# GpSimd computes the low part of a weight slot in four pieces instead of one

## The chip, the cores and the metric

The kernel runs on one core of a Trainium2 chip. The metric is the device time of one execution in microseconds (us); lower is better. The core has five engines that run side by side and meet at semaphores: PE (TensorE, matrix products), DVE (VectorE), ACT (ScalarE), POOL (GpSimd) and SP (SyncE, which here only starts transfers). In the rows, PEld is PE's weight load.

## The reference

Two layers of a hybrid decoder step run over 256 prompt tokens and 64 batch tokens (8 sequences of 8). Cut to the order of the work, a layer is:

```python
x = x + 0.5 * swiglu(rmsnorm(x, ffn1_norm), ffn1_w_gate, ffn1_w_up, ffn1_w_down)
z = rmsnorm(x, mix_norm) @ w_in            # 1024 -> 2048: q | k | v | p | a, g | u, v
att = moba_attention(rms(q), rms(k), v)    # the batch tokens also see 256 cached keys
pool = trailing_means(p, (2, 4, 8, 16)) - p, then a map per group
conv = silu(layernorm(depthwise_conv31(a * sigmoid(g)))) @ conv_pw
gmlp = gelu(u) * (tril(spatial_w) @ rmsnorm(gelu(v)) + spatial_b)
x = x + concat(att, pool, conv, gmlp) @ w_out
x = x + 0.5 * swiglu(rmsnorm(x, ffn2_norm), ffn2_w_gate, ffn2_w_up, ffn2_w_down)
```

All of it is in float32.

## The kernel before

**The products.** Every float32 operand of a large product is split into a high part (rounded to fp32r) and a low part (the rest), and PE adds three products: high by high, high weight by low input, low weight by high input (lines 557, 558 and 560). Weights come in slots of 128 rows by 8 k-tiles of 128 columns (1024 columns; in the down projections 6 or 5 k-tiles). There are four slots, j = 0 to 3, each with a place for the raw weights (`raw`), the high part (`w_hi`) and the low part (`w_lo`). SP loads `raw[j]` when the low part made of its old content is done. ACT rounds it into `w_hi[j]` (line 836) when PE has finished with the slot. Then `w_lo = raw - w_hi` is computed, by DVE (line 1041) for most slots, and by POOL (line 468) for 16 slots of each layer: those of the last three of four iterations of the input projection (`BASE_I`, i = 1 to 3) and those of the first iteration of the output projection (`BASE_O`, i = 0). PE waits for the low part of a slot before its first product with it, and frees the slot after 24 products.

**The layer's middle.** Each engine has its own list of instructions, written out by hand, and no scheduler changes it. Between the last iterations of the input projection and the output projection stand the mixers. On POOL the order is: the 12 slots of the input projection; 16 instructions of the late convolution taps for the batch tokens (lines 485 and 488, the last of which PE's convolution mean, line 663, waits for); the window sums of the pooling mixer (lines 503 to 530); the 4 slots of the output projection.

On DVE, in the order in which they come: the copies of the normed q and k into `q_pad` and `k_all` (lines 1266 and 1267, six of them), the rest of the convolution taps (1153), the softmax of the prompt tokens, the gate's norm (1314, twice), the softmax of the batch tokens (`prob_s` by its inverse sum, 1320, then by a mask into `prob_new`, 1324), a product for the gates (1330), a reciprocal (1335), and the product of the convolution's layer norm (1338, twice), on which ACT's swish (993) waits.

On PE the mixers stand in this order: transposes of the gate values (687), prompt attention (701), transposes of the batch probabilities (731, which wait for line 1324), the spatial gates (710 to 720), batch attention (738, 741), the convolution's pointwise map (765, which waits for the swish of line 993), the pooling map (758), transposes (751), and then the output projection.

Semaphore `split_p` counts the slots that POOL has done: one for each slot. PE and SP both wait on it.

Of the kernel before, what the change touches and what calls it, by code (L numbers as in the profile page):

```python
# [24 lines left out]
F32 = mybir.dt.float32  # L25
F32R = mybir.dt.float32r
I32 = mybir.dt.int32
ALU = mybir.AluOpType
# [3 lines left out]
P = 128  # L32
# [11 lines left out]
DT = D_MODEL // P  # L44
# [41 lines left out]
CONST_LOADS = 2 + len(KEPT) + 4 + 2  # L86
GROUPS = 4

STORED_STEP, HISTORY_STEP = 7, 4
SMALLS = 7  # L90
STATES = 7
# [12 lines left out]
def hybrid_decoder(nc, xT, w8, w11, gains, vecs, consts, pool_w, conv_pw, sp_wT, sp_b,  # L104
# [3 lines left out]
    with ctx:  # L108
        place = [16512]

        def sb(name, shape, dt=F32, at=None):
            n = 4
            for s in shape[1:]:
                n *= s
            offset = place[0] if at is None else at[0]
            t = nc.alloc_sbuf_tensor_at(name, shape, dt, offset=offset)
            end = offset + (n + 31) // 32 * 32
            if at is None:
                place[0] = end
                assert end <= 229344, (name, end)  # L120
            else:
                at[0] = end
                assert end <= at[1], (name, end, at[1])
            return t

        raw = sb("raw", [P, 4, 8 * P])
        w_hi = sb("w_hi", [P, 4, 8 * P], F32R)
        w_lo = sb("w_lo", [P, 4, 8 * P], F32R)
# [93 lines left out]
        def sig(name, per_layer, head=0):  # L222
            return Signal(ctx.enter_context(nc.semaphore(name)), per_layer, head)
# [12 lines left out]
        split_p = sig("split_p", 16)  # L236
# [226 lines left out]
        def _(pool):  # L463
            def split_iteration(L, base, i):

                for j in range(4):
                    pool.wait_ge(split_hi.sem, L * split_hi.per + (base + i) * 4 + j + 1)
                    pool.tensor_tensor(w_lo[:, j, :], raw[:, j, :], w_hi[:, j, :].bitcast(F32), ALU.subtract).then_inc(split_p.sem, 1)  # L468

            def late_history_taps(L):  # L470

# [66 lines left out]
            for L in range(DEPTH):  # L538
                for i in range(1, IT_I):
                    split_iteration(L, BASE_I, i)  # L540
                late_history_taps(L)
                window_sums(L)
                split_iteration(L, BASE_O, 0)
# [973 lines left out]
```

## Time and profile before

| | us |
|---|---|
| median of three runs | 1189.28 |
| the runs | 1186.16, 1189.28, 1194.22 |
| the profiled execution, its own time | 1193.69 |
| its span in the trace | 1191.9 |
| PE busy in the span | 1161.5 (97%) |
| DVE busy | 754.6 (63%) |
| ACT busy | 528.0 (44%) |
| POOL busy | 120.1 (10%), 104 instructions |

The rows come from the profiled execution. Busy times of engines overlap. The three runs lie 8 us apart, which is what a difference has to be read against. Where a row names an engine and a line behind an arrow, the instruction waited for that.

### The profile page before, as it was taken

The page shows a single profiled execution, that of the slowest core. Times are in us where ns is not written, and L with a number is a line of the kernel's source. Part 1 is how long each engine was busy: PE and PEld are TensorE (multiplying, and loading weights), DVE is VectorE, ACT ScalarE, POOL GpSimd, SP SyncE. Part 2 cuts the span into 40 slices and gives each one's busy share as a digit, 9 for nine tenths or more (in the row PEclk, how much of TensorE's full clock was granted, in tenths as well). Part 3 has the DMA queues.
Part 4 walks back from the last instruction along what each step waited for, and adds up shares of the span by engine and source line. Part 5 has one row for each costly group of instructions (what it writes and reads, how often), then busy time and mean ns, then how long its engine had stood idle before and what let it go on. Part 6 is the DMA issues. An engine that isn't in the chain of part 4 may idle for free.

```text
span 1191.9 us, 22460 instructions
## 1 busy us (share of the span) xinstructions
PE 1161.5 (97%) x7920; PEld 1138.6 (96%) x7920; DVE 754.6 (63%) x1225; ACT 528.0 (44%) x778; POOL 120.1 (10%) x104
## 2 busy tenths in 40 slices
PE   5999999999899999999999999999998999999999
PEld 4999999999789999999999999999976999999998
DVE  6667765557967666555566677645778675666442
ACT  4444444444656344444444444444446453444332
POOL 1000000026810000000000000000576000000000
PEclk9999999999999999999999999999998999999999
DMA  7544434567236444435564444455652354444453
GB/s 245 176 143 155 143 114 146 148 195 233 83 107 188 150 150 150 146 111 145 167 205 155 144 151 132 127 153 171 205 189 72 109 173 144 153 146 136 129 151 104
DMA packets 71356, 180.23 MB, mean 151 GB/s; under 512 B 10074, under 2 KB 25234, under 8 KB 71314
## 3 DMA queue, kind: packets, MB, share of 16 engines
q1 hardware_dynamic: 70656, 178.97, 48.2%
q10 hardware_dynamic: 658, 0.73, 0.2%
q8 instruction: 23, 0.38, 0.1%
q14 instruction: 19, 0.16, 0.0%
HBM read 176.09 MB, written 3.58 MB: 151 GB/s over the span
## 4 chain that ended last, share of the span: by engine, by line
PE 91%; DVE 7%; issue 1%; DMA 1%; ACT 0%; SPq 0%; DVEq 0%; ACTq 0%
PE bank L557 30%; PE bank L560 30%; PE bank L558 30%; DVE bank L1153 1%; DMA x<-in_xT 1%; PE bank L765 0%; DVE prob_s L1320 0%; DVE w_lo L1041 0%; DVE xg_lo L1048 0%; DVE prob L1274 0%; DVE q_pad L1266 0%; DVE z_w L1314 0%; PE bank L570 0%; DVE prob L1300 0%; DVE tmp L1309 0%
## 5 line engine op out<-in xcount | busy, mean ns | idle before, releaser
L836 ACT ACTIVATE w_hi<-raw 128x1024 fp32r<-128x1024 f32 (+2 forms) x352 | 337.9, 961 | 464.6 <-PE bank L560 452.5
L557 PE MATMUL bank<-xg_hi,w_hi 128*128 128x320 f32 x1664 | 519.0, 312 | 11.5 <-DVE xg_lo L1048 11.5
L558 PE MATMUL bank<-xg_lo,w_hi 128*128 128x320 f32 x1664 | 515.3, 310 | 0.0
L560 PE MATMUL bank<-xg_hi,w_lo 128*128 128x320 f32 x1664 | 515.3, 310 | 0.0
L1041 DVE TENSOR_TENSOR w_lo<-raw,w_hi 128x1024 fp32r<-128x1024 f32 (+2 forms) x320 | 349.2, 1092 | 159.8 <-ACT w_hi L836 148.9
L557 PEld LDWEIGHTS bank<-xg_hi,w_hi 128*128 128x128 f32 x1664 | 313.6, 188 | 15.3 <-issue 12.4
L558 PEld LDWEIGHTS bank<-xg_lo,w_hi 128*128 128x128 f32 x1664 | 313.6, 188 | 0.9 <-issue 0.2
L560 PEld LDWEIGHTS bank<-xg_hi,w_lo 128*128 128x128 f32 x1664 | 313.4, 188 | 0.0
L557 PE MATMUL bank<-h_hi,w_hi 128*128 128x320 f32 x704 | 217.5, 309 | 0.0
L558 PE MATMUL bank<-h_lo,w_hi 128*128 128x320 f32 x704 | 217.5, 309 | 0.0
L560 PE MATMUL bank<-h_hi,w_lo 128*128 128x320 f32 x704 | 217.5, 309 | 0.0
L468 POOL TENSOR_TENSOR w_lo<-raw,w_hi 128x1024 fp32r<-128x1024 f32 x32 | 78.0, 2455 | 778.1 <-ACT w_hi L836 778.1
L557 PEld LDWEIGHTS bank<-h_hi,w_hi 128*128 128x128 f32 x704 | 132.2, 188 | 0.0
L558 PEld LDWEIGHTS bank<-h_lo,w_hi 128*128 128x128 f32 x704 | 132.2, 188 | 0.0
L560 PEld LDWEIGHTS bank<-h_hi,w_lo 128*128 128x128 f32 x704 | 132.2, 188 | 0.0
L1075 DVE TENSOR_TENSOR tmp<-bank,rms 128x320 f32<-128x320 f32 x88 | 43.2, 491 | 101.8 <-PE bank L560 101.8
L1072 DVE TENSOR_TENSOR tmp<-bank,rms 128x320 f32<-128x320 f32 x88 | 43.2, 491 | 54.2 <-PE bank L560 52.7
L821 ACT ACTIVATE xg_hi<-x,gain 128x320 fp32r<-128x320 f32 (+1 forms) x48 | 26.3, 561 | 82.3 <-DVE x L1098 81.8
L844 ACT ACTIVATE h_hi<-tmp 128x320 f32 (+1 forms) x88 | 41.5, 472 | 21.4 <-DVE tmp L1078 21.4
L1048 DVE SCALAR_TENSOR_TENSOR xg_lo<-x,gain,xg_hi 128x320 fp32r<-128x320 f32 (+1 forms) x48 | 27.2, 579 | 34.6 <-ACT xg_hi L821 34.6
L1078 DVE TENSOR_TENSOR tmp<-tmp 128x320 f32<-128x320 f32 x88 | 43.3, 492 | 5.0
L1153 DVE SCALAR_TENSOR_TENSOR bank<-conv_in,vec,bank 128x256 f32<-128x256 f32 x116 | 46.4, 479 | 0.0
(178 smaller groups left out, 707.9 us busy)
## 6 DMA issues: line engine op xcount, KB each, us to landing
raw<-in_w SPq DMA_DIRECT2D x224, 512.0 KB, 3.8
raw<-in_w SPq DMA_DIRECT2D x64, 384.0 KB, 3.1
raw<-in_w SPq DMA_DIRECT2D x64, 320.0 KB, 2.8
k_all<-in_cache_kT SPq DMA_DIRECT2D x32, 128.0 KB, 2.8
v_past<-in_cache_v SPq DMA_DIRECT2D x32, 128.0 KB, 3.2
x<-in_xT SPq DMA_DIRECT2D x2, 640.0 KB, 5.9
out_yT<-x SPq DMA_DIRECT2D x1, 960.0 KB, 4.9
out_kT<-qk SPq DMA_DIRECT2D x2, 320.0 KB, 4.7
```

Of the source, the lines that this page charges most:

```text
L468: pool.tensor_tensor(w_lo[:, j, :], raw[:, j, :], w_hi[:, j, :].bitcast(F32), ALU.subtract).then_inc(split_p.sem, 1)
L557: pe.matmul(out, hi, in_hi[:, k, :], start=first and n == 0, stop=False)
L558: pe.matmul(out, hi, in_lo[:, k, :], start=False, stop=False)
L560: mm = pe.matmul(out, lo, in_hi[:, k, :], start=False, stop=last and end)
L836: act.activation(w_hi[:, j, 0:count * P], raw[:, j, 0:count * P], ACT.Copy).then_inc(split_hi.sem, 1)
L844: act.activation(h_hi[:, bass.ds(i * 2 + m, 1), :].rearrange("p a t -> p (a t)"), tmp[:, 6 + m, :], ACT.Copy).then_inc(h_hi_ok.sem, 1)
L1041: dve.tensor_tensor(w_lo[:, j, 0:count * P], raw[:, j, 0:count * P], w_hi[:, j, 0:count * P].bitcast(F32), ALU.subtract).then_inc(split_v. ...
L1048: dve.scalar_tensor_tensor(out=xg_lo[:, bass.ds(d, 1), :].rearrange("p a t -> p (a t)"), in0=one, scalar=gain[:, bass.ds(gain_col, 1)], in ...
L1072: dve.tensor_tensor(tmp[:, m, :], bank[2 * m][:, 0:TOK], rms[:, :], ALU.mult).then_inc(taken.sem, 1)
L1075: dve.tensor_tensor(tmp[:, 4 + m, :], bank[2 * m + 1][:, 0:TOK], rms[:, :], ALU.mult).then_inc(taken.sem, 1)
L1078: dve.tensor_tensor(tmp[:, 6 + m, :], tmp[:, 2 + m, :], tmp[:, 4 + m, :], ALU.mult).then_inc(h_ok.sem, 1)
L1153: dve.scalar_tensor_tensor(out=out, in0=conv_in[:, c, bass.ds(k, SEQ)], scalar=vec[:, bass.ds(L * NV + k * GT + (V_CW + c), 1)], in1=conv_ ...
```

## The change

For each of POOL's 32 slots the one subtraction over 1024 columns becomes four subtractions over 256 columns each, in order, with nothing between them. The semaphore is counted by the last one, so that SP and PE are still told once, when the whole slot is done. Nothing else differs: the lists of the other four engines are the same, instruction for instruction.

```diff
+LOW_TILES = 2
...
                 for j in range(4):
                     pool.wait_ge(split_hi.sem, L * split_hi.per + (base + i) * 4 + j + 1)
-                    pool.tensor_tensor(w_lo[:, j, :], raw[:, j, :], w_hi[:, j, :].bitcast(F32), ALU.subtract).then_inc(split_p.sem, 1)
+                    for first in range(0, DT, LOW_TILES):
+                        cols = slice(first * P, (first + LOW_TILES) * P)
+                        low = pool.tensor_tensor(w_lo[:, j, cols], raw[:, j, cols], w_hi[:, j, cols].bitcast(F32), ALU.subtract)
+                    low.then_inc(split_p.sem, 1)
```

## Rows read from the trace of the kernel before

**Rows 1.** The page: the chain that ended last, by engine.

```profile
PE 91%; DVE 7%; issue 1%; DMA 1%; ACT 0%; SPq 0%; DVEq 0%; ACTq 0%
```

**Rows 2.** Groups of POOL instructions by shape: count, busy us, mean ns.

```profile
L468 POOL TENSOR_TENSOR w_lo<-raw,w_hi 128x1024 fp32r<-128x1024 f32 x32 | 78.0, 2455 | 778.1 <-ACT w_hi L836 778.1
...
L485 POOL TENSOR_TENSOR tmp<-conv_in,vec 128x128 f32<-128x128 f32 x16 | 6.5, 407 | 2.5 <-POOL conv_y L488 2.5
L537 POOL TENSOR_TENSOR tmp<-x 128x320 f32<-128x320 f32 x4 | 4.2, 1087 | 8.2 <-DMA x<-in_xT 8.2
...
L526 POOL TENSOR_TENSOR tmp<-tmp,pool_in 128x512 f32<-128x512 f32 x2 | 2.4, 1186 | 0.4 <-POOL tmp L525 0.4
```

**Rows 3.** Timeline of POOL, layer 0: start us, us, engine, line.

```profile
277.96 9.55 POOL L468 TENSOR_TENSOR w_lo<-raw,w_hi 128x1024 fp32r<-128x1024 f32 x4 [5.18 <-ACT w_hi L836]
...
306.87 0.46 POOL L488 TENSOR_TENSOR conv_y<-conv_y,tmp 128x128 f32<-128x128 f32 x1
...
321.70 10.07 POOL L468 TENSOR_TENSOR w_lo<-raw,w_hi 128x1024 fp32r<-128x1024 f32 x4
```

**Rows 4.** Timeline near the program's start, POOL and DVE by turns.

```profile
11.01 0.96 POOL L537 TENSOR_TENSOR tmp<-x 128x320 f32<-128x320 f32 x1
11.31 1.00 DVE L1048 SCALAR_TENSOR_TENSOR xg_lo<-x,gain,xg_hi 128x320 fp32r<-128x320 f32 x1
...
11.93 0.96 POOL L537 TENSOR_TENSOR tmp<-x 128x320 f32<-128x320 f32 x1
```

**Rows 5.** Timeline of layer 0's middle: four DVE rows and one of POOL.

```profile
321.03 1.06 DVE L1314 SCALAR_TENSOR_TENSOR z_w<-z_w,vec,tmp 128x320 f32<-128x320 f32 x2
...
322.19 2.67 DVE L1320 TENSOR_TENSOR prob_s<-prob_s,stat 128x528 f32<-128x528 f32 x1
324.89 2.33 DVE L1324 TENSOR_TENSOR prob_new<-prob_s,cst 128x128 f32<-128x128 f32 x1
...
329.65 2.87 DVE L1338 TENSOR_TENSOR conv_y<-conv_y,tmp 128x320 f32<-128x320 f32 x2
...
327.04 4.73 POOL L468 TENSOR_TENSOR w_lo<-raw,w_hi 128x1024 fp32r<-128x1024 f32 x2
```

**Rows 6.** Timeline of DVE at the same place of layer 1.

```profile
904.33 3.24 DVE L1314 SCALAR_TENSOR_TENSOR z_w<-z_w,vec,tmp 128x320 f32<-128x320 f32 x2
...
907.68 2.68 DVE L1320 TENSOR_TENSOR prob_s<-prob_s,stat 128x528 f32<-128x528 f32 x1
910.40 2.31 DVE L1324 TENSOR_TENSOR prob_new<-prob_s,cst 128x128 f32<-128x128 f32 x1
...
915.13 0.89 DVE L1338 TENSOR_TENSOR conv_y<-conv_y,tmp 128x320 f32<-128x320 f32 x2
```

**Rows 7.** Timeline of PE: what it waited for before each, in brackets.

```profile
313.74 1.34 PE L663 MATMUL bank<-conv_y,ones 128*128 128x320 f32 x4 [0.88 <-DVE conv_y L1153]
...
327.28 0.44 PE L731 MATMUL bank<-cst,prob_s 128*128 128x128 f32 x2 [1.43 <-DVE prob_new L1324]
...
334.86 2.39 PE L765 MATMUL bank<-conv_y,w_pw 128*128 128x320 f32 x8 [1.52 <-ACT conv_y L993]
...
907.72 0.63 PE L687 MATMUL bank<-cst,z_w 128*128 128x128 f32 x4 [0.95 <-DVE z_w L1314]
...
912.77 0.44 PE L731 MATMUL bank<-cst,prob_s 128*128 128x128 f32 x2 [2.47 <-DVE prob_new L1324]
...
922.74 3.10 PE L765 MATMUL bank<-conv_y,w_pw 128*128 128x320 f32 x8
```

**Rows 8.** Stretches from:to, length, busy us of PE, PEld, DVE, ACT, POOL, granted clock.

```profile
330.00:333.00 3.00, 3.00 (x38) 1.52 (x36) 3.00 (x4) 1.38 (x3) 1.77 (x1) 1.00 0.59 197
916.00:918.00 2.00, 2.00 (x16) 1.18 (x18) 1.53 (x5) 1.97 (x4) 0.00 (x0) 0.50 0.59 201
```

**Rows 9.** Timeline of layer 1: POOL's last input-projection slot, and DVE.

```profile
879.45 2.41 POOL L468 TENSOR_TENSOR w_lo<-raw,w_hi 128x1024 fp32r<-128x1024 f32 x1 [2.21 <-ACT w_hi L836]
...
879.85 2.43 DVE L1266 COPY q_pad<-qk 64x64 f32<-64x64 f32 x2
```

## The prediction

> **What bounds the kernel now.** I read the page's chain first: PE holds 91% of it and DVE 7% [rows 1]. So the time is PE's products, plus the places where PE waits, and nearly all of these lie in the mixers, where DVE is the engine that ends last. POOL is on no link of the chain, and in the list of waits no row of another engine has POOL as its releaser: no low part comes too late. By that reading alone a change to POOL's subtraction would be worth nothing. What decides is another reading: how long DVE's instructions take while POOL is busy.
>
> The timeline of layer 0's middle gives it. POOL begins its four output-projection slots at 321.70 and ends them at 331.77 [rows 3]. In that time DVE's line 1320 takes 2.67 us, line 1324, over 128 columns, takes 2.33 us, and the two of line 1338 take 2.87 [rows 5]. In layer 1 POOL is done before line 1338 starts, and there the same two take 0.89 [rows 6]. Line 1314 is the reverse case: 1.06 us for two in layer 0, begun before POOL's slots, and 3.24 in layer 1, begun beside them [rows 5, 6]. The ends fit a lock: line 1324 ends at 324.89 + 2.33 = 327.22, just after POOL's third slot starts at 327.04, that is, after the second ended [rows 5]. Each of these DVE instructions reads two tiles of SBUF, or copies one, and it stands still until the POOL instruction in progress is over. POOL's instruction is 2.4 us long, so that is what a DVE instruction can lose.
>
> PE pays. It waits 1.43 us for line 1324 and 1.52 us for the swish that follows line 1338 in layer 0; in layer 1 0.95 us for line 1314 and 2.47 us for line 1324 [rows 7].
>
> **The pieces.** The change removes 32 instructions of 2.455 us and adds 128 over 256 columns. No row shows such a piece. It can hardly cost less than a quarter of the whole, 2.455 / 4 = 0.61 us, and hardly more than two of 128 columns, 2 x 0.407 = 0.81 us [rows 2]. Between the rows of 128 and 512 columns it comes to 0.407 + 128/384 x (1.186 - 0.407) = 0.67 us, and this I take, since both rows are subtractions or products of two tiles on the same engine. A slot is then 2.68 us (2.44 to 3.24) in place of 2.4, the length that four in a row show, 9.55 / 4 [rows 3].
>
> That cost lies beside other work. SP and PE are told at the end of a slot as before, 0.3 us later. The seven last input-projection slots come one after the other from 277.96, so that the late taps behind them end up to 7 x 0.3 = 2 us after their 307.33 of now, and the product that needs them starts at 313.74, after a wait for DVE and not for POOL [rows 3, 7]. The cover there is 6.4 us. The output-projection slots end near 334 with the time they give up to DVE. The projection's first column comes only after the pointwise map, 334.86 + 2.39 [rows 7], less the 3 us that this may move, and reads the first of the four; the other three follow at a column each. So I charge nothing for the pieces. If the cover were gone, the charge would be 0.3 us for each slot in the queue.
>
> **The shorter hold.** A DVE instruction now waits for at most one piece, 0.67 us. Layer 0: lines 1320 and 1324 take 327.22 - 322.19 = 5.03 us. Alone, by the rate of line 1338 (0.89 us for 640 columns), they need at most 0.73 + 0.45 = 1.2 us; with two full pieces 2.5. They end at least 2.5 us earlier, and PE, which waits 1.43 us for them, loses that wait whole. Line 1338 is then asked for earlier by as much, and takes at most 0.89 + 1.34 = 2.23 us; it ends more than 3 us earlier, and ACT's swish before the pointwise map moves with PE's transposes. The second wait, 1.52, goes too. What comes last then is PE's own list of mixer products. **Layer 0: -2.95 us**; that is all PE can gain there.
>
> Layer 1: from line 1314 to the end of line 1324 there are 912.71 - 904.33 = 8.4 us. Alone these need about 1.06 + 0.15 + 1.2 = 2.4, with three pieces 4.4. The 4.0 us saved cover PE's two waits, 0.95 + 2.47. **Layer 1: -3.42 us.**
>
> **The granted clock.** In layer 1 PE goes slower after those waits: the clock is 0.50, the 1.2 GHz level, in a stretch where layer 0 has 1.00 [rows 8]. From line 731 to line 765 it needs 9.97 us, and in layer 0 7.58 with a wait of 1.52 in it, so 6.06; line 765 to its end is 3.10 against 2.39 [rows 7]. That is 3.9 + 0.7 = 4.6 us more. Before the fall PE stood idle for 2.47 us, which layer 0 did not have. Without that wait I expect layer 1 to look like layer 0, so that **-4.6 us** come on top in an execution in which the clock fell.
>
> **The copies.** At the end of the input projection six DVE copies meet POOL's last slot. In layer 1 POOL starts at 879.45 and DVE asks at 879.85; the first two copies take 2.43 us [rows 9]. With pieces the first copy goes in early, but the next three each meet another piece, in place of a tap of 0.41 us. Three times 0.67 - 0.41 is 0.8 us more, and the first wait is 1.7 us shorter, while the POOL work ahead of the taps is the same: between -0.5 and +0.8 us for each layer, and I put 0.
>
> **The sum.** Against the profiled execution: 1193.69 - 2.95 - 3.42 - 4.6 = 1182.7. The median of the runs is 4.4 us below that execution; if the clock fell there in fewer places, only the part without it comes off: 1189.28 - 6.4 = 1182.9. Both say **1183**.
>
> **A rule that speaks against it.** The rows at the start of the program show POOL with four products of 320 columns and no wait between them, and DVE with a row of products: they go by turns, 0.92 us from one POOL start to the next, and each is near 1 us long [rows 4], where such a DVE product alone takes 0.53 [rows 5]. So DVE does come between two POOL instructions that nothing separates. The Trainium skill, "GPSIMD Engine Reference", section "Instruction dispatch", says that a POOL core begins the next instruction as soon as its share of the last is finished, with nothing to hold it back. By that, four pieces without a wait might keep DVE out as one does, and the time would stay at 1189. The Trainium skill, "SBUF — State Buffer", section "Who interferes with whom", has the lock held for one instruction, which these rows bear out.
>
> **The rivals.** First, nothing changes: POOL keeps the tiles from DVE over all four pieces. For it: pieces have no semaphore between them, which the slots had. Against it: the turns at the start [rows 4]. It gives 1189 (1186 to 1192).
>
> Second, the clock counts in full: the three runs had the fall that the profile shows, and it is gone. Then 1189.28 - 11.0 = 1178.3. For it: the waits before the fall go. Against it: the median lies below the profiled execution.
>
> Third, slower: POOL becomes late. If a piece cost as much as the four products of 320 columns on the page, 1.09 us [rows 2], a slot would be 4.35, and seven of them end 7 x 1.95 = 13.6 us later than now, past the 6.4 us of cover at the convolution mean: about +7 us a layer on the chain, 14 together, against gains that halve with so long a hold, some 3. That is 1200. It decides from a slot of 2.4 + 6.4 / 7 = 3.3 us on, a piece of 0.83. Against it: those four took turns with DVE, so that 1.09 holds DVE's time too, and pieces of a full 1.09 would need DVE's requests without a break.
>
> **How the numbers follow.** The forecast, 1183, has 0.58; the clock in full 0.22; nothing 0.12; POOL late 0.05; 0.03 is left for what I don't see. The range takes in half of the mixers' gain lost to the copies and to POOL's new times (1189) and nearly all of the clock case (1177). With runs 8 us apart, about 1%, or 12 us, is what a measurement of this kernel can tell from no change: faster by over 1% is below 1177.4, a part of the clock case, 0.13; slower by over 1% is above 1201, half of POOL late and the unseen, 0.04; the rest, 0.83, is within.
>
> **What the profile of the changed kernel would show.** 128 POOL subtractions of 0.6 to 0.8 us; in layer 0 lines 1320 and 1324 (four lines further down now) together below 2.6 us in place of 5.0, and line 1338 near 1 us for one; the waits of 1.43, 1.52, 0.95 and 2.47 us on PE gone or below 0.5; a granted clock of 1.00 after the transposes of layer 1. If the DVE rows are still 2.3 us long, the first rival holds. If they are short and PE waits as long, the chain ran elsewhere and I mistook it. If the convolution mean waits for POOL, the pieces cost more than I think.

## The result, and the profile after

| | before | after |
|---|---|---|
| median of 5 runs, us | 1189.63 | 1181.75 |
| the runs | 1186.16 to 1194.22 | 1180.56 to 1183.82 |
| the profiled execution | 1193.69, span 1191.9 | 1180.56, span 1178.8 |

The ratio is 0.9935, with a 95% interval of 0.9912 to 0.9957: 7.9 us, or 0.65%, faster. The runs also lie closer together than before. The profiled execution of before lies near the top of its range and that of after at the bottom, so that the two traces are 13.1 us apart, and not 7.9.

The pieces first. This is the page's row for POOL's slots after the change (count, busy us, mean ns of one); it answers to [rows 2]. Lines up to 468 are where they were, and those of the engines behind them stand four lines further down.

```profile
L471 POOL TENSOR_TENSOR w_lo<-raw,w_hi 128x256 fp32r<-128x256 f32 x128 | 91.4, 749 | 761.5 <-ACT w_hi L840 761.5
```

A piece takes 0.749 us, where 0.67 was said. The timeline of POOL, layer 0, gives the slots (start us, us); it answers to [rows 3]:

```profile
276.71 14.02 POOL L471 TENSOR_TENSOR w_lo<-raw,w_hi 128x256 fp32r<-128x256 f32 x20 [4.64 <-ACT w_hi L840]
...
297.68 2.79 POOL L471 TENSOR_TENSOR w_lo<-raw,w_hi 128x256 fp32r<-128x256 f32 x4 [2.67 <-ACT w_hi L840]
...
308.76 0.46 POOL L492 TENSOR_TENSOR conv_y<-conv_y,tmp 128x128 f32<-128x128 f32 x1
...
324.47 11.80 POOL L471 TENSOR_TENSOR w_lo<-raw,w_hi 128x256 fp32r<-128x256 f32 x16
```

A slot is 14.02 / 5 = 2.80 us in place of 2.39. The late taps end at 309.22 and not 307.33, and the output slots begin 2.8 us later than before, although everything around them is earlier. Lateness was in the prediction (up to 2 us for the taps), but not what it does to DVE. The timeline of DVE, layer 0, against [rows 5]:

```profile
296.11 0.41 DVE L1270 COPY q_pad<-qk 64x64 f32<-64x64 f32 x2
...
312.52 2.57 DVE L1304 TENSOR_TENSOR prob<-prob,stat 128x512 f32<-128x512 f32 x2
...
318.62 1.21 DVE L1318 SCALAR_TENSOR_TENSOR z_w<-z_w,vec,tmp 128x320 f32<-128x320 f32 x2
...
319.94 0.79 DVE L1324 TENSOR_TENSOR prob_s<-prob_s,stat 128x528 f32<-128x528 f32 x1
320.76 0.29 DVE L1328 TENSOR_TENSOR prob_new<-prob_s,cst 128x128 f32<-128x128 f32 x1
...
323.84 1.01 DVE L1342 TENSOR_TENSOR conv_y<-conv_y,tmp 128x320 f32<-128x320 f32 x2
```

Lines 1324 and 1328 (1320 and 1324 before) take 1.08 us together in place of 5.0. But they are over at 321.05, 3.4 us before POOL's slots start at 324.47, and the copies at 296.11 are over before the last input slot starts at 297.68. So in layer 0 the long rows are gone because DVE and POOL no longer meet. Of the rows shown only line 1342 ran partly beside pieces. In layer 1 it is closer, but the same; timeline of DVE against [rows 6], then POOL's output slots:

```profile
899.02 1.50 DVE L1324 TENSOR_TENSOR prob_s<-prob_s,stat 128x528 f32<-128x528 f32 x1
900.55 0.29 DVE L1328 TENSOR_TENSOR prob_new<-prob_s,cst 128x128 f32<-128x128 f32 x1
```

```profile
900.98 12.06 POOL L471 TENSOR_TENSOR w_lo<-raw,w_hi 128x256 fp32r<-128x256 f32 x16
```

Line 1328 ends at 900.84, just before the slots begin. The profile alone can't tell the shorter hold from the later slots, and the first experiments are for that.

The timeline of PE, both layers, against [rows 7]:

```profile
318.75 0.66 PE L635 MATMUL bank<-cst,z_v 128*128 128x128 f32 x4 [1.74 <-DVE z_v L1148]
...
323.37 0.44 PE L735 MATMUL bank<-cst,prob_s 128*128 128x128 f32 x2
...
329.37 2.42 PE L769 MATMUL bank<-conv_y,w_pw 128*128 128x320 f32 x8
...
898.04 0.65 PE L635 MATMUL bank<-cst,z_v 128*128 128x128 f32 x4 [2.08 <-DVE z_v L1148]
...
904.29 0.44 PE L735 MATMUL bank<-cst,prob_s 128*128 128x128 f32 x2
...
910.28 2.42 PE L769 MATMUL bank<-conv_y,w_pw 128*128 128x320 f32 x8
```

The four waits of the prediction (1.43, 1.52, 0.95 and 2.47 us) are gone. From the transposes to the pointwise map layer 1 needs 910.28 - 904.29 = 5.99 us, where it needed 9.97. A wait for `z_v`, the gate values, stands in both layers now, 1.74 and 2.08 us. Where the clock fell in layer 1, the stretches show (length, busy us of PE, PEld, DVE, ACT, POOL, granted clock); they answer to [rows 8]:

```profile
900.00:904.00 4.00, 4.00 (x31) 3.14 (x30) 3.62 (x5) 2.62 (x5) 3.88 (x7) 0.61 0.00 0
904.00:908.00 4.00, 4.00 (x47) 2.79 (x48) 2.09 (x5) 3.57 (x9) 4.00 (x6) 1.00 0.45 135
```

The clock still falls to its lower level (0.50 from 900 to 903), but for some 3 us, right behind the wait for `z_v`, and not over the batch attention.

To see where the span's 13.1 us went, I take two marks of PE in each layer: the start of the transposes of q and k, and the first product of the output projection. Timeline of PE before:

```profile
299.04 2.11 PE L623 MATMUL bank<-qk 64*128 64x128 f32 x16
...
338.52 0.39 PE L557 MATMUL bank<-mix_hi,w_hi 128*128 128x320 f32 x1
...
881.51 2.11 PE L623 MATMUL bank<-qk 64*128 64x128 f32 x16
...
927.11 0.39 PE L557 MATMUL bank<-mix_hi,w_hi 128*128 128x320 f32 x1
```

The same marks after:

```profile
297.78 2.12 PE L627 MATMUL bank<-qk 64*128 64x128 f32 x16
...
333.05 0.39 PE L561 MATMUL bank<-mix_hi,w_hi 128*128 128x320 f32 x1
...
876.03 2.11 PE L627 MATMUL bank<-qk 64*128 64x128 f32 x16
...
913.97 0.39 PE L561 MATMUL bank<-mix_hi,w_hi 128*128 128x320 f32 x1
```

Layer 0's middle went from 39.48 to 35.27 us, layer 1's from 45.60 to 37.94: 4.2 and 7.7 us. Between the layers, and behind the second, nothing changed (543.0 us in both kernels, and 264.8 in both). The remaining 1.3 us lie ahead of the first mark: PE's sums of squares for layer 0's mixer norm (`mix_norm`) started at 254.36 before and 253.10 now, and POOL's first changed instruction starts at 255.39, so these 1.3 us are not the change's. In these two executions all the rest lies in the two middles, as forecast. How much of it is the change's own they can't say: they lie 5 us further apart than the medians.

### The profile page after: what moved, and what is told of

It reads as the page before. It is cut to its first block, busy times and chain, and to the rows that moved or that the text cites. A ratio compares the mean times of both kernels' runs of the same rounds, so it can differ in the third digit from the quotient of the medians.

```text
span 1178.8 us, 22556 instructions
## 1 busy us (share of the span) xinstructions
PE 1155.3 (98%) x7920; PEld 1135.3 (96%) x7920; DVE 744.4 (63%) x1225; ACT 528.2 (45%) x778; POOL 135.1 (11%) x200
## 4 chain that ended last, share of the span: by engine, by line
PE 93%; DVE 6%; DMA 1%; issue 0%; ACT 0%; SPq 0%; DVEq 0%; ACTq 0%
PE bank L561 30%; PE bank L564 30%; PE bank L562 30%; DVE bank L1157 1%; DMA x<-in_xT 1%; DVE prob L1304 0%; DVE w_lo L1045 0%; DVE xg_lo L1052 0%; PE bank L769 0%; DVE prob L1278 0%; DVE tmp L1313 0%; PE bank L745 0%; PE bank L705 0%; DVE sumsq L1060 0%; DVE qk L1264 0%; PE bank L574 0%
## 5 line engine op out<-in xcount | busy, mean ns | idle before, releaser
L471 POOL TENSOR_TENSOR w_lo<-raw,w_hi 128x256 fp32r<-128x256 f32 x128 | 91.4, 749 | 761.5 <-ACT w_hi L840 761.5
```

The source lines that it names most:

```text
L471: low = pool.tensor_tensor(w_lo[:, j, cols], raw[:, j, cols], w_hi[:, j, cols].bitcast(F32), ALU.subtract)
```

## The experiments

My theory: a DVE instruction that reads or copies SBUF waits for the POOL instruction in progress, and pieces make that wait short. The rival that the profile raised: POOL is later, so that DVE passes first. Ratios are against the kernel before, with 95% intervals. All kernels compute all of the reference.

### Pieces only where DVE was seen to wait

```diff
-                    for first in range(0, DT, LOW_TILES):
-                        cols = slice(first * P, (first + LOW_TILES) * P)
+                    tiles = LOW_TILES if base == BASE_O or (i, j) == (IT_I - 1, 3) else DT
+                    for first in range(0, DT, tiles):
+                        cols = slice(first * P, (first + tiles) * P)
```

Five slots of a layer are in pieces, the last of the input projection and the four of the output projection; the other eleven are whole, so that the pieces don't make POOL late there.

> Pieces only where POOL's slots lie beside DVE's row: the last input-projection slot and the four output-projection slots of a layer; the other 11 input slots whole, so that POOL is not made late. The theory of the hold (a DVE instruction waits for 0.7 us instead of 2.4) expects nearly the whole gain: about 1183 us, the lines 1320 and 1324 of before together below 2.6 us though POOL's output slots start as early as before, and PE's four waits gone. The theory of the lateness (the pieces cost 0.4 us a slot, reloads and the last slots of the stage come 3 to 4 us later, and DVE's instructions pass before POOL starts) expects little: 1187 to 1190, since nothing is late.

Measured: 1182.12 us (8 runs, 1179.86 to 1184.72), ratio 0.9929 (0.9904 to 0.9954), as much as the whole change. Layer 1 is the better test here, since DVE's instructions run beside POOL's pieces. Timeline of DVE (five lines further down than before):

```profile
901.54 1.04 DVE L1325 TENSOR_TENSOR prob_s<-prob_s,stat 128x528 f32<-128x528 f32 x1
902.61 0.70 DVE L1329 TENSOR_TENSOR prob_new<-prob_s,cst 128x128 f32<-128x128 f32 x1
...
905.74 1.53 DVE L1343 TENSOR_TENSOR conv_y<-conv_y,tmp 128x320 f32<-128x320 f32 x2
```

And POOL's output slots there:

```profile
901.04 12.80 POOL L472 TENSOR_TENSOR w_lo<-raw,w_hi 128x256 fp32r<-128x256 f32 x16
```

From 901.04 on POOL works without a break, and the two softmax products begin in that row and still need 1.04 and 0.70 us, where beside whole slots they needed 2.68 and 2.31 [rows 6]. This is the shorter hold, seen by itself: each loses at most 0.4 us against the 0.71 and 0.29 that they take with POOL idle (in the first kernel with a wait, below). POOL in turn gives time up: its sixteen pieces take 12.80 us in place of 16 x 0.70. In layer 0 of this execution DVE passes ahead of POOL, as in the kernel after: the two products are over at 322.62, and the output slots begin at 325.00, although the eleven slots are whole.

### Pieces only where DVE was not seen to wait

The condition turned round: `tiles = LOW_TILES if base == BASE_I and (i, j) != (IT_I - 1, 3) else DT`. Eleven slots in pieces, the five that meet DVE whole. POOL is meant to be late, and the hold is long.

> The other part alone: pieces at the first 11 input-projection slots of a layer, whole slots at the last one and at the output projection. The hold expects 1188 to 1191, with DVE instructions still held for up to 2.4 us. The lateness expects 1182 to 1185: the copies into q_pad at 0.2 us each, ahead of POOL's last input slot, and the output slots 3 to 4 us later, past the lines 1320 and 1324 of before, but perhaps in the way of line 1338.

Measured: 1187.07 us (12 runs, 1183.81 to 1196.41), ratio 0.9984 (0.9958 to 1.0011): not to be told from no change. Timeline of DVE, layer 1:

```profile
901.35 2.67 DVE L1325 TENSOR_TENSOR prob_s<-prob_s,stat 128x528 f32<-128x528 f32 x1
904.05 2.33 DVE L1329 TENSOR_TENSOR prob_new<-prob_s,cst 128x128 f32<-128x128 f32 x1
...
908.80 2.86 DVE L1343 TENSOR_TENSOR conv_y<-conv_y,tmp 128x320 f32<-128x320 f32 x2
```

In layer 1 PE waits 1.4 us for the first two and 1.5 for the swish, as in layer 0 before. Layer 0 of the same execution is another case. Timeline of DVE there, then POOL's output slots in both layers:

```profile
321.19 0.79 DVE L1325 TENSOR_TENSOR prob_s<-prob_s,stat 128x528 f32<-128x528 f32 x1
322.01 0.29 DVE L1329 TENSOR_TENSOR prob_new<-prob_s,cst 128x128 f32<-128x128 f32 x1
...
325.24 4.72 DVE L1343 TENSOR_TENSOR conv_y<-conv_y,tmp 128x320 f32<-128x320 f32 x2
```

```profile
324.68 10.07 POOL L472 TENSOR_TENSOR w_lo<-raw,w_hi 128x1024 fp32r<-128x1024 f32 x4
...
900.85 10.06 POOL L472 TENSOR_TENSOR w_lo<-raw,w_hi 128x1024 fp32r<-128x1024 f32 x4
```

The two products pass before the slots, and PE has neither the wait for them nor the one for the swish. From the transposes of q and k to the first output product layer 0 needs 35.52 us, as little as the kernel after (35.27), with whole slots. So where POOL comes late enough, lateness does what the pieces do. But the pieces at the eleven slots don't bring it about. Counted from the transposes of q and k, the output slots of layer 1 start at 22.87 us here, and at 22.66 (layer 0) and 23.12 (layer 1) before: the last input slot waits for ACT in any case (0.91 us here), which takes the lateness up. Over the runs no gain shows.

### Whole slots, made as late

Here the kernel before is given 128 columns more to subtract, into a tile that nobody reads, at those eleven slots. It is more work for POOL with no piece anywhere.

```diff
+                    if base == BASE_I and (i, j) != (IT_I - 1, 3):
...
+                        low = pool.tensor_tensor(late[:, :], raw[:, j, 7 * P:], w_hi[:, j, 7 * P:].bitcast(F32), ALU.subtract)
```

> No pieces at all: the first 11 input-projection slots of a layer each get an additional subtraction over 128 columns into a tile that nothing reads, about 0.4 us, which makes POOL as late as the pieces do. The hold expects no gain: 1189 to 1191. The lateness expects 1182 to 1185, the same as with pieces at these slots.

Measured: 1189.68 us (12 runs, 1183.64 to 1197.01), ratio 1.0004 (0.9977 to 1.003). In layer 1 the two products take 2.67 and 2.33 us, with the output slots 22.78 us behind the transposes of q and k; in layer 0, with the slots at 26.05, they take 0.79 and 0.29, and PE has neither wait there. So more work at the eleven slots brings nothing over the runs, in pieces or not, and the gain of the change comes from the five slots that meet DVE. What lateness at the output slots would be worth by itself these two kernels don't show, since in layer 1 they don't have it.

### No pieces, but POOL waits for DVE

If the meeting is what costs, whole slots that start behind DVE's products must bring as much. In the first kernel POOL waits for DVE's `prob_new` before the output slots; in the second for the six copies before the last input slot as well.

```diff
+                pool.wait_ge(s_norm.sem, s_norm.at(L, 3))
```

> Whole slots as before the change; POOL only waits for the masked batch probabilities (line 1324 of before) ahead of its four output-projection slots, so that lines 1314, 1320 and 1324 run free; the copies still meet the last input slot, and line 1338 may meet a whole output slot. If the output slots are most of the price, 1183 to 1185; if the copies are worth as much, about 1186.

> No pieces and no additional work: POOL waits for the six copies ahead of its last input slot, and for the masked batch probabilities (line 1324 of before) ahead of its output slots, so that the collisions are avoided by order alone. Both theories expect a gain here, 1181 to 1184, if the collisions of POOL's slots with DVE are the whole price; a time near 1189 would say that neither has the cause. The hold alone would leave line 1338 of layer 0 held by a whole slot, up to 2.4 us, with up to 1 us of it on PE.

Measured: 1182.29 us, ratio 0.9925 (0.9902 to 0.9947), and 1182.69 us, ratio 0.9932 (0.9908 to 0.9956). So one wait for four slots a layer gives what 128 pieces give. DVE in the first of them, layer 1:

```profile
877.12 1.93 DVE L1267 COPY q_pad<-qk 64x64 f32<-64x64 f32 x2
...
902.41 0.71 DVE L1321 TENSOR_TENSOR prob_s<-prob_s,stat 128x528 f32<-128x528 f32 x1
903.15 0.29 DVE L1325 TENSOR_TENSOR prob_new<-prob_s,cst 128x128 f32<-128x128 f32 x1
...
906.35 4.77 DVE L1339 TENSOR_TENSOR conv_y<-conv_y,tmp 128x320 f32<-128x320 f32 x2
```

The convolution's products lose 3.9 us to whole slots, more than in the kernel before (2.87 us for the two), and PE's list has no wait for the swish behind them: asked for early enough, they have that much room. PE's second wait of layer 0 was thus a consequence of the first delay, and not of line 1338's own length. In the second kernel the copies take 0.41 us for two in both layers, and it is not faster. PE's lists of waits say why; first the kernel with one wait, then the one with both:

```profile
PE bank L649 <- DVE prob L1275: 3.4, 2, 1.9
...
PE bank L632 <- DVE z_v L1145: 2.6, 2, 1.3
PE bank L664 <- DVE conv_y L1154: 1.8, 2, 0.9
```

```profile
PE bank L634 <- DVE z_v L1147: 4.1, 2, 2.1
```

(Line, releaser, us in all, times, the longest.) With the copies out of the way the waits behind them go, and PE stands longer at `z_v`. The medians show nothing for the copies' hold.

### The size of a piece

`LOW_TILES` 4 and 1 in place of 2: two pieces of 512 columns, eight of 128.

> Every slot in two pieces of four k-tiles: a hold of about 1.25 us. Lines 1320 and 1324 together need up to 1.2 + 2 x 1.25 = 3.7 us in place of 5.0; the wait of 1.43 us on PE nearly goes and that of 2.47 in layer 1 mostly. If the gain goes with the hold, 1183 to 1186, between whole slots and four pieces.

> Every slot in eight pieces of one k-tile. The hold falls to 0.4 us, but PE waits for DVE in none of the four places any more with four pieces, so the hold has no more to give; a slot costs about 8 x 0.41 = 3.3 us, and seven in a row come 6 us later than before the change, just inside the cover of 6.4 us at the convolution mean. 1181 to 1184, with PE's convolution mean waiting for POOL if the cover is used up.

Halves: 1182.07 us, ratio 0.9927 (0.9897 to 0.9957), a slot of 2.55 us. No worse than quarters, although single DVE rows are longer (2.53 us for the second two copies into `q_pad` of layer 1): the waits have room for it. Eighths: 1186.55 us (12 runs, 1182.96 to 1191.49), ratio 0.9958 (0.9935 to 0.9981). Nearly half of the gain is lost, and not as I had thought: in the profiled execution PE waits for POOL at the convolution mean in neither layer. That execution took 1191.49 us, the longest of the twelve, so the long rows in it need not stand in the others. Timeline of DVE:

```profile
333.88 7.64 DVE L1344 TENSOR_TENSOR mix_lo<-tmp,mix_hi 128x320 fp32r<-128x320 f32 x2 [1.99 <-ACT mix_hi L1001]
...
883.27 4.86 DVE L1270 COPY q_pad<-qk 64x64 f32<-64x64 f32 x2
...
921.42 1.53 DVE L1344 TENSOR_TENSOR mix_lo<-tmp,mix_hi 128x320 fp32r<-128x320 f32 x2 [1.99 <-ACT mix_hi L1001]
```

and of POOL beside it:

```profile
326.89 13.87 POOL L471 TENSOR_TENSOR w_lo<-raw,w_hi 128x128 fp32r<-128x128 f32 x32
...
864.13 23.57 POOL L471 TENSOR_TENSOR w_lo<-raw,w_hi 128x128 fp32r<-128x128 f32 x56 [3.77 <-ACT w_hi L840]
...
911.10 15.10 POOL L471 TENSOR_TENSOR w_lo<-raw,w_hi 128x128 fp32r<-128x128 f32 x32
```

The two copies end at 883.27 + 4.86 = 888.13, and POOL's row of 56 pieces at 887.70; the two `mix_lo` end at 341.52, and POOL's row of 32 at 340.76. The first copy of the pair took 4.49 us of it and the first product 7.24. DVE got in only when the row was over, or nearly. That is the mechanism of the prediction's first rival, POOL keeping the tiles over all its pieces, and with pieces of 128 columns it does occur; but not each time: the same `mix_lo` in layer 1 took 1.53 us in the midst of 32 pieces. For the starved one PE waited 3.70 us at 341.26.

### Eighths without lateness, with and without a wait between them

Eighths only at the five slots that meet DVE; in the second kernel each piece also waits on a semaphore for the one before.

```diff
+                        if first:
+                            low.then_inc(piece.sem, 1)
+                            pool.wait_ge(piece.sem, n)
```

> Eight pieces, but only where POOL meets DVE (the last input slot and the output slots of a layer); the other slots whole, so that lateness is out. If eighths lost their gain in the run with eight pieces everywhere because POOL came late, this gives 1181 to 1183. If POOL keeps DVE out over a row of short pieces (the copies waited 4.5 us there, the gate's low part 7.2 us), single DVE rows of 3 us and more stay beside the pieces, and the time is 1183 to 1188, with a wide spread.

> The same eight pieces at the same slots, each one now waiting for the one before it, as the window sums do, which leaves POOL idle for about 0.2 us between two. If the row of short pieces without a wait keeps DVE out, no DVE row beside them is longer than its own work and 0.5 us, and the time is 1181 to 1183 although a slot takes 4.7 us; if it is only the number of pieces or their length, nothing changes against the run without these waits.

Measured: 1182.69 us, ratio 0.9924 (0.9896 to 0.9953), and 1181.76 us, ratio 0.9921 (0.9894 to 0.9948). Neither profile has a long DVE row beside the pieces (1.54 us for two `mix_lo` at most), so the pair can't tell whether a wait is what lets DVE in. In the second, PE waited 0.67 us for POOL at the convolution mean of layer 0. Where all slots are in eighths, the starved rows stood in the longest row of pieces, and in one of 32; the same row of 32 does no harm in layer 1 or here. What decides it stays open, and so does how much of the loss in eighths is due to it.

### What PE waits for now

In the kernel after, PE waits 1.74 and 2.08 us for `z_v`. Ahead of it DVE has line 1304, two softmax products that take 2.57 us in layer 0 and 3.30 in layer 1 beside POOL's window sums. So I took the kernel with five slots in pieces and let POOL wait for that softmax after its third window sum; then also for the copies, as above.

```diff
+                pool.wait_ge(p_norm.sem, p_norm.at(L, 3))
```

> Pieces where POOL meets DVE (the last input slot and the output slots), as in the run of the hold alone, and POOL also waits for the prompt softmax (line 1300 of before) ahead of the fourth of its window sums, so that this product, held by POOL for about 0.9 us, runs free. PE's wait for the next tile of the projection, 1.7 us in each layer with pieces, should fall by about that: 1180 to 1182, if POOL's later end stays hidden; 1183 or more if the output projection waits for it.

> The fastest version so far (four pieces at the last input slot and the output slots, and the window sums waiting for the prompt softmax), in which POOL also waits for the six copies ahead of its last input slot. In executions in which POOL comes early the copies, 2.8 us with pieces, would fall to 1.2 us: 1177 to 1178.5. No change, 1178 to 1179, if POOL's last input slot mostly comes behind the copies anyway.

Measured: 1178.40 us (6 runs, 1177.29 to 1180.38), ratio 0.989 (0.9855 to 0.9926), and 1178.13 us (6 runs, 1176.76 to 1178.63), ratio 0.9887 (0.986 to 0.9914). The softmax product and PE's wait in the first:

```profile
892.72 1.83 DVE L1306 TENSOR_TENSOR prob<-prob,stat 128x512 f32<-128x512 f32 x2
```

```profile
PE bank L637 <- DVE z_v L1150: 2.0, 2, 1.0
```

Line 1306 takes 1.83 us and the wait is 1.0 us in each layer. Both kernels beat the one before by more than the change does: their ranges lie below that of the change, 1180.56 to 1183.82, though the first by only 0.2 us, and the intervals of the ratios overlap. The two can't be told from each other; the copies again bring nothing that shows.

## Why the prediction was right, point by point

**The time.** 1183 was said, and 1181.75 measured. The second rival, the clock in full (1178.3), lies below all five runs. That the figure came so near is in part luck, as the parts below show.

**The pieces.** 0.67 us was taken, 0.61 to 0.81 were the bounds, 0.749 it is; the slot is 2.80 and not 2.68 us. The cover held, and the third rival, POOL late, did not come. Its bound, a slot of 3.3 us, was too strict: with eighths a slot takes 3.37 us, and PE waited for POOL in neither layer. The step takes the last seven slots to come one after the other, but only the first four do [rows 3]; the other three waited 0.46, 1.99 and 1.37 us for ACT, and this is room for longer slots. What the step missed is that POOL's times also move with the loads. ACT waits 2.63, 2.42 and 4.41 us for the raw weights of the last three input slots of layer 0, and POOL's last one starts at 297.68 although PE is 1.3 us earlier. That is not the pieces' doing: with the eleven slots whole, in the first experiment, ACT waits 3.45, 1.81 and 3.46 us there. Why the loads come later than in the trace of before stays open.

**The shorter hold.** The cause is shown: pieces at the five slots that meet DVE bring the whole gain, pieces or more work at the other eleven none that shows, and a wait in place of the pieces the same gain. So what costs is DVE meeting a long instruction of POOL, and that a piece holds DVE for less is seen in layer 1 of the first experiment. The four waits on PE are gone. But in the profiled execution of the kernel after, lines 1324 and 1328 were over before POOL's output slots began, in both layers, so there it was the order that spared them; in how many executions they meet pieces, one trace can't say. Layer 0's middle gave 4.2 us where 2.95 were put, since its waits for `prob` (1.17 us at line 648) and for the convolution mean (0.88) went too, and 0.4 and 0.5 came new. So "all PE can gain there" was wrong. And it can't all be put down to the change, since layer 0 is as short in the trace with whole output slots (35.52 us). For layer 1 the sum was 3.42 + 4.6 = 8.0, and 7.7 were measured. That line 1338 had to become short for the second wait of layer 0, as the step has it, was needless: it came earlier, and that was enough.

**The granted clock.** In the profiled execution the 4.6 us of the step came as said: 9.97 - 5.99 = 3.98, and 3.10 - 2.42 = 0.68 at the pointwise map. The statement that layer 1 would then be like layer 0 was too much, for behind the wait for `z_v` the clock fell again, for a shorter time. From the start of line 673, 899.10, to line 735 layer 1 needs 5.19 us, where layer 0 needs 323.37 - 319.81 = 3.56. That 1.6 us is balanced by as much at line 648 and the one behind it, 656, where the products of layer 1 took 3.20 and 1.79 us before (2.02 and 1.34 in layer 0) and take 2.02 and 1.34 now. In the runs, all those of before have a mean granted clock of 0.9948 and a mean time of 1190.6; the five of after 0.9982 and 1181.9. Among the runs of before 0.001 of clock goes with 1.15 us. By that, 3.9 of the 8.7 us go with the clock and 4.8 are left for the waits, where the median's sum put 6.4 and no clock. So 1183 from 1189.28 - 6.4 was right in its total with its parts shifted. This is a relation between runs, in which waits and clock may move together, and was not tried by itself.

**The copies.** 0 was put, with -0.5 to +0.8 for each layer. On DVE they became shorter by 1.6 and 1.4 us, more than the bound, because POOL's later slot let most of them pass. On PE's side 0 agrees with the medians: the experiment that frees them in whole shows no gain over the one that doesn't.

**The rule that speaks against it.** With pieces of 256 columns the traces agree with the turns at the start [rows 4]: DVE comes in between two pieces. With 128 columns it sometimes did not. The Trainium skill, "GPSIMD Engine Reference", section "Instruction dispatch", has a core begin the next instruction as soon as its share of the last is finished. What the prediction drew from that, DVE kept out over the row, came at times with 128 columns and in no trace with 256. So the first rival was false for this change but is no empty case.

## What to carry to other kernels

An engine that is on no link of the chain can still set its length through an engine that shares something with it: look for rows of DVE that take far longer at one place than the same line elsewhere, and for the GpSimd instruction that ends when they end. Compare more than one trace or layer before putting a shorter row down to a change: the two engines may just not have met. Cutting that instruction into two or four pieces bounds the loss, and a single wait that lets DVE go first does as much for less; with either, the gain ends where the next wait stands, which is the place to look next. Don't cut finer than needed: eight pieces at every slot gave up nearly half of the gain, and in one trace unwaited rows of them kept DVE out.

## What was not expected of the hardware

With eighths at all slots, a DVE copy and a DVE product took 4.49 and 7.24 us, where alone they take 0.2 and 0.45, while POOL ran its own instructions of 0.42 us one after another without a wait, and they ended within 0.4 us of the end of that row. The Trainium skill, "SBUF — State Buffer", section "Who interferes with whom", has the shared ports held for one instruction. The rows shown here beside slots of 1024 columns and pieces of 256 agree (2.67 and 1.04 us for the same product, 0.71 alone), and these two do not. The price of a GpSimd subtraction is not in proportion to its columns: 0.42 us at 128, 0.70 to 0.75 at 256, 1.27 at 512 and 2.39 at 1024, so that the slot grows from 2.39 to 2.55, 2.80 and 3.37 us with two, four and eight pieces.
